# One 128-row weight transfer issued as eight transfers of eight rows and one of 64

## The reference, cut to what matters

```
hh = xb @ w1[e] + b1[e]                 # xb: tokens of expert e, w1[e]: 1024 x 2048
y  = swiglu_clamped(hh) @ w2[e] + b2[e] # w2[e]: 1024 x 1024
out = sum over the 4 experts of a token of gate * y
```

## Time and profile before

| what | value |
|---|---|
| median of three runs | 1452.96 us |
| the profiled execution's own time | 1450.59 us |
| its span, first to last instruction | 1448.7 us |
| PE busy | 1306.1 us (90%) |
| VectorE busy, ScalarE busy | 532.9 us (37%), 400.9 us (28%) |
| transfers: moved, mean rate | 508.45 MB, 351 GB/s |
| mean granted PE clock | 0.983 |

### The profile page before, as it was taken

The page is one execution under the profiler, slowest core; times in us unless marked ns, Lnnn a source line. Parts: engine busy times, 40 slices in busy tenths (PEclk is TensorE's granted clock), DMA queues, the critical chain, the costliest instruction groups (busy, mean ns, idle before and its releaser), DMA issues.

```text
span 1448.7 us, 32671 instructions
## 1 busy us (share of the span) xinstructions
PE 1306.1 (90%) x13166; PEld 791.9 (55%) x13166; DVE 532.9 (37%) x1085; ACT 400.9 (28%) x745; POOL 0.2 (0%) x4
## 2 busy tenths in 40 slices
PE   9999999999999988999999799887997879988896
PEld 8998679998688653343444234332443324433343
DVE  6833678785597752112121121111211202111122
ACT  6734444553455641111111011111110101111112
POOL 0000000000000000000000000000000000000000
PEclk9999999999999999999999899999999999999999
DMA  9431975455773599999999999999999999999996
GB/s 365 175 118 59 402 314 207 183 193 204 256 324 118 210 392 427 433 425 391 435 423 430 433 426 429 434 424 431 434 424 429 437 422 430 434 426 426 434 424 257
DMA packets 28893, 508.45 MB, mean 351 GB/s; under 512 B 3232, under 2 KB 3360, under 8 KB 4640
## 3 DMA queue, kind: packets, MB, share of 16 engines
q1 hardware_dynamic: 28800, 507.08, 83.6%
HBM read 506.02 MB, written 1.05 MB: 350 GB/s over the span
## 4 chain that ended last, share of the span: by engine, by line
PE 61%; DMA 24%; DVE 7%; ACT 5%; issue 3%; SPq 0%; DVEq 0%; ACTq 0%
PE acc L1300 20%; DMA low<-in_w 15%; PE acc L532 9%; PE acc L1319 8%; DMA high_part<-in_w 7%; PE acc L1290 3%; PE acc L1257 3%; PE acc L995 2%; PE acc L570 2%; DMA low<-in_stream 2%; PE acc L1264 1%; PE acc L571 1%; DVE w_lo L1499 1%; ACT high_part L1916 1%; PE acc L915 1%
## 5 line engine op out<-in xcount | busy, mean ns | idle before, releaser
L1300 PE MATMUL acc<-low,high_part 128*32 128x512 f32 x2384 | 290.5, 618 | 56.0 <-DMA low<-in_w 43.9
L2502 DVE TENSOR_SCALAR high_part<-acc 128x256 f32<-128x256 f32 x53 | 22.5, 425 | 509.9 <-PE acc L1300 509.9
L1300 PEld LDWEIGHTS acc<-low,high_part 128*32 128x32 f32 x2384 | 88.8, 113 | 216.2 <-issue 161.4
L1319 PE MATMUL acc<-low,high_part 128*32 128x256 f32 x2624 | 151.2, 381 | 7.7 <-DMA low<-in_w 7.7
L1914 ACT ACTIVATE high_part<-high_part 128x256 f32<-128x256 f32 x53 | 22.1, 417 | 473.0 <-DVE high_part L2502 473.0
L1499 DVE TENSOR_TENSOR w_lo<-low,w_hi 128x4096 fp32r<-128x4096 f32 (+1 forms) x30 | 130.5, 4352 | 36.3 <-ACT w_hi L1493 35.9
L1300 PE MATMUL acc<-high_part 128*32 128x512 f32 x1008 | 118.9, 598 | 12.1 <-DMA high_part<-in_w 8.7
L1319 PEld LDWEIGHTS acc<-low,high_part 128*32 128x32 f32 x2624 | 82.5, 110 | 70.0 <-issue 15.5
L1493 ACT ACTIVATE w_hi<-low 128x4096 fp32r<-128x4096 f32 (+1 forms) x28 | 99.7, 3568 | 56.6 <-DMA low<-in_stream 51.2
L1290 PE MATMUL acc<-high_part 32*128 32x256 f32 x864 | 77.1, 425 | 14.9 <-ACT high_part L1931 11.5
L532 PE MATMUL acc<-x_hi,w_hi 128*128 128x256 f32 x352 | 85.4, 284 | 0.8 <-DVE x_lo L1527 0.7
(11 more groups left out here) (494 smaller groups left out, 1824.7 us busy)
## 6 DMA issues: line engine op xcount, KB each, us to landing
low<-in_w SPq DMA_DIRECT2D x53, 4096.0 KB, 33.4
high_part<-in_w SPq DMA_DIRECT2D x51, 2048.0 KB, 32.6
low<-in_stream SPq DMA_DIRECT2D x41, 2048.0 KB, 8.2
low<-in_w SPq DMA_DIRECT2D x34, 2048.0 KB, 23.1
high_part<-in_stream SPq DMA_DIRECT2D x4, 2048.0 KB, 12.0
high_part<-in_natb SPq DMA_DIRECT2D x1, 2048.0 KB, 13.7
low<-in_w SPq DMA_DIRECT2D x2, 1024.0 KB, 41.6
high_part<-in_rows SPq DMA_DIRECT2D x1, 1536.0 KB, 14.0
```

What stands on the lines that cost most here:

```text
L1300: last = mm(flat[32 * q:32 * q + 32, 2048:2560], XG[:, b, 32 * kk:32 * kk + 32], wp[:, 2048 * b + 512 * q:2048 * b + 512 * q + 512], start ...
L1319: last = mm(flat[32 * q:32 * q + 32, 2816:3072], AT[:, 128 * (c % 2) + 32 * (c // 2):128 * (c % 2) + 32 * (c // 2) + 32], wp[:, 1024 * (c ...
L2502: ts(GLU, flat[:, 2048:2304], 7.0, None, ALU.min).then_inc(S("glu"), 1)
```

## The change

In `expert_piece`, piece n = 190 is no longer one transfer of 128 rows. It is eight transfers of eight rows each, four rows apart (rows 0, 4, 8, ..., 28, then 1, 5, ..., 29, and so on, then the same from row 32 on), which together cover rows 0 to 63, and one transfer of rows 64 to 127. Each of the nine adds 16 to the slot's semaphore, and PE's wait for this piece asks for 128 more. Bytes, destination, order against the other pieces, and all compute stay as they are.

```
             def expert_piece(e, n):
 
                 r = EXPERT_PIECES[n][1]
+                if n == 6 * NE - 2:
+                    for row in (0, 1, 2, 3, 32, 33, 34, 35):
+                        rows = slice(row, row + 29, 4)
+                        sp.dma_start(slot_of(n)[rows, :], w2[bass.ds(1 * e, 1), rows, 0:NPIECE].rearrange("a p n -> (a p) n"))\
+                          .then_inc(S(f"slot{n % NSLOT}_loaded"), 16)
+                    sp.dma_start(slot_of(n)[P // 2:P, :], w2[bass.ds(1 * e, 1), P // 2:P, 0:NPIECE].rearrange("a p n -> (a p) n"))\
+                      .then_inc(S(f"slot{n % NSLOT}_loaded"), 16)
+                    return
                 if n == 6 * NE - 1:
...
-                    pe.wait_ge(S(f"slot{s}_loaded"), 16 * (slot_base[s] + count))
+                    parts = P // 16 if n == 6 * NE - 2 else 0
+                    pe.wait_ge(S(f"slot{s}_loaded"), 16 * (slot_base[s] + count + parts))
```

## The result

The changed kernel takes 1462.99 us (median of 4 runs, 1461.53 to 1464.36) against 1452.92 for the one before, timed beside it (1451.81 to 1454.37). The ratio is 1.0071, 95% interval 1.0058 to 1.0085: slower by 10.1 us. The forecast was 1452.4. The profiled execution of the changed kernel took 1461.53, span 1459.8, mean granted clock 0.976 (before: 1450.59, 1448.7, 0.983). The new transfers are L398 (eight rows) and L400 (64 rows).

What follows compares the result with a forecast made beforehand. The weight stream's late engines were taken to bound the end, with PE losing 0.54 to 0.64 us; 0.54 + 0.06 = 0.6 us less takes the median from 1452.96 to 1452.4, range 1450.8 to 1455.6.

Steps and rivals of the forecast that it cites:

- What bounds the kernel: Last 12 us: PE loses 0.54 to 0.64 us to transfers; eight engines end 6 to 8 us after the first.
- The bytes: Piece 190: 0.61 us per row, so the deciding engine has 4 rows fewer, the same or more; took -2.44 us.
- worst row: Three 256 KB transfers issued from 367.2 to 368.1: landings 0.95 us apart for 0.61 of bytes, 0.34 us each.
- rival C: Each new transfer costs its engine something; at 0.34 us each, last matmuls start 0.6 us later: 1453.6, chance 0.06.
- The late eight: End of the stream: guessed that the late engines get 4 rows fewer, ending at 1434.0 instead of 1436.5.
- rival A: Late engines carry 12 rows; landings of pieces 190 and 191 come 2.44 us later: 1455.4, chance 0.18.
- PE and SP: Last matmuls: PE can use only 0.6 of 2 us won; SP's eight more issues, 4 us, cost 0.
- Price of a transfer: Eight more transfers on the loaded engines: 0 to 2.7 us, taken as 0.1.
- B: Piece 190's rows stay evenly dealt over the engines, landings as before: 1452.96, chance 0.07.
- D: Eight short transfers on one engine go singly, each confirmed first, 12 us in all: about 1462.9, chance 0.04.
- E: Rival A plus 1.2 GHz clock after its 2.2 us wait, 5.1 us more: 1460.5, chance 0.02.
- The signs: DMA share near 1.00 until about 1431 supports the forecast; about half from 1426 to 1428.5, lasting to 1439, supports rival A.

Runs made afterwards that it cites:

- extra_low: Kernel before plus eight unread eight-row transfers, rows 0-63, 2048 columns, ahead of whole piece 190; cost not told from 0, at most 1.9 us.
- every_second: Kernel before with piece 190 as two transfers of 64 rows, even rows then odd; 428 GB/s where they are written, kernel time unchanged.
- columns: Kernel before with piece 190 as eight transfers of all 128 rows, 512 columns each; 1452.7 us.

## Why the prediction was wrong

**What bounds the kernel: right.** The three views gave the end correctly: waits of 0.5 to 0.6 us, all of it for the stream, and eight engines that end 6 to 8 us behind the first. That the gain could be 0.6 us at most was right for that execution. For others it was generous. In the profiled execution of before PE's wait of 2.95 us for weights at 1358.31 was not followed by a fall of the clock, and the 16 matmuls took 1.92 us. The same point in the changed kernel:

```profile
1359.68 3.53 PE L1308 MATMUL acc<-high_part 128*32 128x512 f32 x16 [2.81 <-DMA high_part<-in_w]
```

It is not the change's doing, as it lies 35 us before the first of its transfers is issued; in extra_low and every_second it reads the same. Such an execution reaches piece 188 about 3 us later (1428.96 against 1425.98) and then waits less for the stream: extra_low had 0.19 and 0.27 us. Of the 3.0 us upstream, 1.6 are this half clock (3.53 against 1.92) and 1.4 stood already before it (1359.68 against 1358.31). It is a reason why the gain would hardly have been there.

**The bytes: the step that failed.** It read "The 64-row transfer deals 4 rows to each of 16 engines", priced 0.61 us each, so that the only question was which eight engines get 12 rows and which 4 (-2.44, 0 or +2.44 us). The dealing is as said: the share is 1.00 for 64 rows, and 0.50 for eight. But 0.61 us is the time of a row when the 16 engines write all over the 128 partitions, and the prediction carried the figure over to a transfer that writes one half. There it is 1.28 us, and up to 1.95 while others write to the same half. It left a bound open on how the small transfers are dealt, and none on how long a row of the 64-row one takes.

The trace of before held a warning, in the very transfers that the prediction took for its worst row. L378 writes 256 KB three times, each to only 32 partitions. The stretch of before in which the transfer ahead of them ends, and the one in which most of their bytes move:

```profile
370.00:372.00 2.00, 2.00 (x10) 1.62 (x10) 0.00 (x0) 0.00 (x0) 0.00 (x0) 1.00 1.11 373
372.00:374.00 2.00, 2.00 (x11) 1.62 (x10) 0.00 (x0) 1.54 (x1) 0.00 (x0) 1.00 0.94 209
```

A share of 0.94 with 209 GB/s is half the rate on busy engines. The packets of 8 KB, 0.31 us each around 370, take 0.6 to 0.65 from 372 to 373. The prediction read the landings 0.95 us apart as a price of 0.34 us per transfer (rival C). They were slower rows.

**The late eight and the halves of the rows.** The prediction took the split by lateness and the split by rows to be the same one, as a guess. Which engines are loaded doesn't decide the sign: the change costs +10.1 us and its mirror image +14.7, where the guess and rival A had -0.6 and +2.4. Whether the guess about the late eight was right stays open.

**PE and SP.** That a landing 2.3 us ahead of need can't be turned into time was right in kind. But piece 189 was not in the sum, since the prediction let a transfer act only on what is queued behind it. SP's issues cost nothing, as said, though they start 0.85 us apart and not 0.5, and hold piece 191 back by 6 us and not 4.

**Price of a transfer: right as far as measured** (0.1 us for eight; for columns and extra_low the upper ends of the intervals leave at most 2.0 and 1.9 us for all eight). The 2.0 us that the prediction quotes from the Trainium skill stand in a section on transfers issued by GpSimd, and these come from SP.

**The rivals.** A, B and C gave 1455.4, 1453.0 and 1453.6. D gave 1462.9, which is the time measured, and for a reason that is refuted: by themselves the eight small transfers run at 192 GB/s, eight engines at a share of 0.50 of 16 and so without pauses, and as an addition they cost their rows. A time that fits is no proof of its mechanism. E's fall of the clock behind a wait came true, behind the wait for piece 189 (0.58 from 1434 to 1438), at 1.35 us and not 5.1.

**The signs.** The share "falls to about one half already at 1426 to 1428.5" was to show rival A. It stayed at 0.99, while the GB/s fell to 139. The prediction listed only the share, and the share alone shows nothing here. Its sign of a wrong forecast, a wait before piece 190, did come, at 2.22 us.

**The sum again, with the sizes measured:** waits 6.75 and 1.55 for the half clock and the broken stretch, less the 0 to 0.6 us of waits that are there before, gives 7.7 to 8.3 of the 10.1 us between the medians. About 2 us are left. Executions of the kernel before differ by up to 2.8 us from their median, and the profiled ones lie 2.3 and 1.5 us under theirs; beyond that these 2 us are not accounted for.

## What to carry to other kernels

In these runs the partitions that a transfer writes set its rate, far more than how many transfers there are: cut a 2048 KB block by columns or by every second row and the kernel's time doesn't change, cut it at row 64 and it runs at half speed and brakes what is in flight beside it. When a trace is read for the price of a transfer that it doesn't contain, look at share and GB/s together: here a full share at half the rate was a collision where the bytes arrive. Where the engines of a queue lie apart, as here by 6 to 8 us, a slow transfer hits the pieces ahead of it too, so the sum must start at the oldest piece still under way.

## What the runs showed of the hardware

- A transfer of 64 rows is not slow as such: 430 GB/s on every second partition, 204 on partitions 64 to 127, 207 on 0 to 63. The Trainium skill ("SBUF — State Buffer", section "Can I just issue two DMAs to hit both halves?") says that only a transfer that spans all 128 partitions reaches all ports and that two half transfers serialize. For the first part, 64 rows are enough if they are spread over the 128 partitions. The second understates it: two halves in series would be 4.9 us more, and cost 13.9.
- 1024 KB written to one half cost the stream 13.1 us, the same bytes over every second partition 2.2.
- Eight adjacent rows run at 66 GB/s at a share of 0.46, eight rows four apart at 192 at 0.50, with the same number of engines.
- A packet of a row took 0.61 us in free flight, mostly 1.1 to 1.3 where writers to one half met and up to 1.95 in the worst stretch.
- The share of the engines can read well over 1.00 (1.14 and 1.15) in stretches where the rate has begun to fall.
- SP took 0.85 us from one eight-row issue to the next, where those at the start of the kernel were 0.45 apart; eight 128-row transfers of 256 KB held it 28.5 us at no cost.
